# A trunk with two grouped MoE layers: passes of 64 tokens on two strips or 32 on four, freed tiles passed on by GpSimd, loops over experts

## What is computed

```python
def grouped_moe(h, router_w, router_b, w_gate, w_up, w_down):
    ...
    w_top, i_top = lax.top_k(in_group, TOP_K)
    w_top = w_top / w_top.sum(-1, keepdims=True)
    ...
    def expert_block(args):
        xb, e = args
        return (jax.nn.silu(xb @ w_gate[e]) * (xb @ w_up[e])) @ w_down[e]
```

## Time and profile before

| | |
|---|---|
| median of 3 runs | 1560.64 us (1557.62 to 1577.38) |
| the profiled execution | 1577.98 us, its span 1576.0 us |
| TensorE, matmuls | 1200.0 us busy (76%), 12964 |
| VectorE / ScalarE / GpSimd | 328.5 / 209.1 / 20.7 us busy |
| HBM | 492 MB read, 313 GB/s over the span |
| mean granted clock of TensorE | 0.833 |
| chain that ended last | PE 62%, DMA 19%, issue 13%, DVE 4% |
| MoE stages | about 230 to 738 us and 1036 to 1557 us of the span |

### The profile page before, as it was taken

One profiled execution on the slowest core, in us unless ns is written; L12 is line 12 of the kernel. 1 busy time (PEld: TensorE's weight loads), 2 busy tenths in 40 slices (PEclk: granted clock), 3 DMA queues, 4 the chain that ended last, 5 costly groups with the idle time before them and its releaser, 6 DMA issues.

```text
span 1576.0 us, 28851 instructions
## 1 busy us (share of the span) xinstructions
PE 1200.0 (76%) x12964; PEld 681.6 (43%) x12964; DVE 328.5 (21%) x838; ACT 209.1 (13%) x409; POOL 20.7 (1%) x53
## 2 busy tenths in 40 slices
PE   3799978667787478749798999677596887468746
PEld 1674344334443245324557565334253444235323
DVE  0595341001111011102400331521010110011004
ACT  0003001001111011102001121111011111111101
POOL 2100000000000000000000000000000000000000
PEclk8899968879888788878799867668798998689867
DMA  9729769999779998999733402159997699988980
GB/s 378 297 90 422 315 284 423 422 424 409 298 299 424 421 422 343 425 418 413 309 135 140 178 0 102 58 222 421 423 377 288 253 391 423 422 373 365 420 340 28
DMA packets 49384, 496.32 MB, mean 315 GB/s; under 512 B 4231, under 2 KB 4247, under 8 KB 8988
## 3 DMA queue, kind: packets, MB, share of 16 engines
q1 hardware_dynamic: 48176, 490.75, 75.3%
q10 hardware_dynamic: 684, 2.32, 0.4%
q0 software_dynamic: 320, 0.16, 0.1%
HBM read 492.17 MB, written 1.05 MB: 313 GB/s over the span
## 4 chain that ended last, share of the span: by engine, by line
PE 62%; DMA 19%; issue 13%; DVE 4%; ACT 1%; ACTq 0%; POOL 0%; DVEq 0%; POOLq 0%
PE PS L852 27%; DMA ring<-in_w_gate_dram 9%; PE PS L748 5%; DMA ring<-in_w_down_dram 5%; PE PS L1010 4%; PE PS L766 4%; DMA ring<-in_w_up_dram 3%; PE PS L887 3%; PE PS L682 3%; PE PS L830 3%; DMA work<-in_conv_ln_b_dram 2%; PE PS L1125 1%; PE PS L1128 1%; PE PS L1131 1%; PE PS L732 1%
## 5 line engine op out<-in xcount | busy, mean ns | idle before, releaser
L852 PE MATMUL PS<-ring,work 128*32 128x256 f32 x8064 | 517.1, 410 | 153.1 <-issue 118.4
L852 PEld LDWEIGHTS PS<-ring,work 128*32 128x32 f32 x8064 | 271.0, 117 | 367.3 <-issue 194.7
L830 PE MATMUL PS<-hs,work 128*32 128x256 f32 x752 | 60.4, 439 | 111.5 <-issue 109.8
L1352 DVE TENSOR_TENSOR work<-work,PS 128x256 f32<-128x256 f32 x47 | 19.8, 421 | 454.5 <-PE PS L852 454.5
L748 PE MATMUL PS<-ring,work 128*128 128x512 f32 x192 | 83.1, 593 | 0.5 <-ACT work L641 0.5
L830 PEld LDWEIGHTS PS<-hs,work 128*32 128x32 f32 x752 | 25.8, 121 | 132.6 <-issue 118.3
L887 PE MATMUL PS<-work 32*128 32x256 f32 x752 | 68.1, 484 | 14.9 <-issue 14.9
L682 PE MATMUL PS<-ring,crep 128*32 128x512 f32 x448 | 61.0, 694 | 18.9 <-DVE crep L1403 11.4
L1347 DVE COPY work<-PS 128x256 f32<-128x256 f32 x47 | 19.9, 424 | 244.0 <-PE PS L842 244.0
L526 ACT ACTIVATE work<-PS 128x256 f32<-128x256 f32 x47 | 18.1, 384 | 373.7 <-PE PS L830 373.7
L852 PE MATMUL PS<-work 128*32 128x256 f32 x960 | 59.7, 396 | 6.3 <-DMA work<-in_w_down_dram 6.3
(11 more groups left out here) (209 smaller groups left out, 853.8 us busy)
## 6 DMA issues: line engine op xcount, KB each, us to landing
ring<-in_w_gate_dram SPq DMA_DIRECT2D x64, 2048.0 KB, 25.5
ring<-in_w_up_dram SPq DMA_DIRECT2D x54, 2048.0 KB, 24.0
ring<-in_w_down_dram SPq DMA_DIRECT2D x54, 2048.0 KB, 21.3
ring<-in_w_ada_dram SPq DMA_DIRECT2D x24, 2048.0 KB, 19.0
work<-in_w_up_dram SPq DMA_DIRECT2D x10, 2048.0 KB, 18.9
work<-in_w_down_dram SPq DMA_DIRECT2D x10, 2048.0 KB, 24.9
ring<-in_w_pw_dram SPq DMA_DIRECT2D x6, 2048.0 KB, 39.3
ring<-in_w_ada_kv_dram SPq DMA_DIRECT2D x4, 2048.0 KB, 14.9
```

The source lines that it names most:

```text
L830: last = pe.matmul(PS[SLOTS * q:SLOTS * (q + 1), X_BANK, 0:QUART], G[:, t, :], hs[:, t, q * QUART:(q + 1) * QUART], start=(t == 0), stop=( ...
L852: last = pe.matmul(dst[SLOTS * s:SLOTS * (s + 1), :], rows[:, cc, SLOTS * q:SLOTS * (q + 1)], quarter(load + h, kk, KH)[:, QUART * s:QUART ...
L1352: dve.tensor_tensor(hh[kind.tile], hh[kind.tile], kind.up, ALU.mult).then_inc(hh_ready, 1)
```

## The change

A block has 64 slots (`large`) or 32 (`small`). An expert with b blocks of 32 by the old count runs `large` b // 2 times and, if b is odd, `small` once at the end. In `large` 64 tokens are the stationary operand and two column strips make 512 output columns each. In `small` 32 tokens are, on four strips: gate and up are made at once, two strips each; in the down product the strips split the columns in two and the contraction in two, and `combine` adds the parts up. TensorE's code holds one `large` and one `small` for each expert, for all experts in turn; ScalarE, VectorE and GpSimd have the bodies once a layer, in a loop over the experts (`Fori(0, E)`), and take the expert's columns by a register.

SP loads the tiles of an expert in the order gate 0, up 0, gate 1, up 1, down 0, down 1, and `large` and `small` use them in that order; the down tiles now have the row layout of the others. TensorE signals `half_done`, `gate_up_done`, `half_down` and `down_done` in every pass. GpSimd waits for each of them at an expert's last pass and raises `tile_free` by two, two, one and one, on which SP's loads into slots of expert tiles wait. The combine of the pass before always runs behind the first product or half, also at the first pass, where `yb` and `GWT` are cleared in advance; behind the last expert the tokens of a column of zeros are gathered once more. Four matmuls of one column close the sums. The diff, cut to its core (the removed bodies are printed above):

```diff
-SLOTS = 32
-STRIPS = 4
+SMALL = 32
+LARGE = 64
...
-    down_h = w_down.rearrange("l e (h q p c) f -> (l e) h p q c f", h=2, q=2, c=2)
+    down_h = w_down.rearrange("l e (h p k) f -> (l e) h p k f", h=2, p=P)
...
-                    sp.wait_ge(half_free, earlier[index] + 1)
+                    before_it = range(earlier[index] + 1)
+                    of_experts = sum(layer_of(i) is not None for i in before_it)
+                    if layer_of(earlier[index]) is None:
+                        sp.wait_ge(half_free, len(before_it) - of_experts)
+                    else:
+                        sp.wait_ge(tile_free, of_experts)
+                sp.dma_start(slot(index).rearrange("p (k f) -> p k f", k=source.shape[1]),
+                             source).then_inc(landed[home[index]], 16)
...
-                    for m, w in enumerate((gate_h, up_h, down_h)):
-                        for h in range(2):
-                            load(index + 6 * e + 2 * m + h, w[l * E + e, h])
+                    for m, (w, h) in enumerate(((gate_h, 0), (up_h, 0), (gate_h, 1), (up_h, 1),
+                                                (down_h, 0), (down_h, 1))):
+                        load(index + 6 * e + m, w[l * E + e, h])
...
+            def free_tiles(l):
+                pool.wait_ge(routed, l + 1)
+                with pool.Fori(0, E) as e:
+                    blocks = pool.value_load(blocks_i[0:1, bass.ds(e, 1)], min_val=1, max_val=SEQ // SMALL)
+                    pool.reg_add(passes, passes, (blocks + 1) // 2)
+                    for signal, tiles in ((half_done, 2), (gate_up_done, 2), (half_down, 1), (down_done, 1)):
+                        pool.wait_ge(signal, passes)
+                        pool.sem_inc(tile_free, tiles)
+
+            free_tiles(0)
             pool.wait_ge(spread_used, SPREADS0)
             for r, w in enumerate((ln_mix_g, ln_mix_b, ln_ffn_g, ln_ffn_b)):
                 pool.dma_start(lnrows[32 * r:32 * r + 1, :], w[1:2, :]).then_inc(rows_in[1], 16)
+            free_tiles(1)
...
+                def large():
+                    n = act.snap(n_act) + 1
                     act.wait_ge(gate_done, n)
+                    act.activation(hh, PS[:, GATE_BANK, :], ACT.Silu).then_inc(sil_ready, 1)
+                    take_x(n + 1)
                     act.wait_ge(hh_turned, n)
+                    act.activation(hhT, PS[:, HT_BANK, :], ACT.Copy).then_inc(hhT_copied, 1)
                     act.wait_ge(down_done, n)
+                    act.activation(yb, PS[:, DOWN_BANK, :], ACT.Copy).then_inc(yb_copied, 1)
                     act.reg_add(n_act, n_act, 1)
 
...
+                with act.Fori(0, E) as e:
+                    blocks = act.value_load(blocks_i[0:1, bass.ds(e, 1)], min_val=1, max_val=SEQ // SMALL)
                     with act.If(blocks > 1):
+                        with act.Fori(0, blocks // 2):
+                            large()
+                    with act.If(blocks % 2 > 0):
+                        small()
...
+                def sum_x(n):
+                    pe.wait_ge(G_built, n + l)
                     for t in range(TT):
+                        for h in range(2):
+                            last = pe.matmul(PS[LARGE * h:LARGE * (h + 1), X_BANK, :], G[:, t, :],
+                                             hs[:, t, h * HALF:(h + 1) * HALF], start=(t == 0), stop=(t == TT - 1),
+                                             tile_position=(0, LARGE * h), skip_group_check=True)
                     last.then_inc(X_summed, 1)
...
+                def combine(n):
+                    pe.wait_ge(yb_copied, n + l + 1)
+                    pe.wait_ge(GWT_copied, n + l + 1)
                     for t in range(TT):
+                        for h in range(2):
+                            pe.matmul(PS[:, 2 * t + h, :], GWT[LARGE * h:LARGE * (h + 1), t * P:(t + 1) * P],
+                                      yb[LARGE * h:LARGE * (h + 1), :], start=False, stop=False,
                                       skip_group_check=True)
+                def columns(tile, k, half):
+                    return quarter(tile, k, KH)[:, half * BANK:(half + 1) * BANK]
+                def large(load):
+                    n = pe.snap(n_pe) + 1
+                    def product(tile, h, bank, signal):
+                        arrived(tile)
+                        for kk in range(KH):
+                            for half in range(2):
+                                last = pe.matmul(PS[LARGE * half:LARGE * (half + 1), bank, :],
+                                                 XT[:, kk, LARGE * h:LARGE * (h + 1)], columns(tile, kk, half),
+                                                 start=(h == 0 and kk == 0), stop=(h == 1 and kk == KH - 1),
+                                                 tile_position=(0, LARGE * half), skip_group_check=True)
+                        if signal is not None:
+                            last.then_inc(signal, 1)
+                    pe.wait_ge(XT_copied, n + l)
+                    product(load, 0, GATE_BANK, None)
+                    combine(n - 1)
+                    product(load + 1, 0, UP_BANK, half_done)
+                    product(load + 2, 1, GATE_BANK, gate_done)
+                    product(load + 3, 1, UP_BANK, gate_up_done)
+                    sum_x(n + 1)
+                    pe.wait_ge(hh_ready, n)
...
+                    last.then_inc(hh_turned, 1)
+                    turn_gw(n)
+                    turn_x(n + 1)
                     pe.wait_ge(hhT_copied, n)
+                    for h in range(2):
...
+                    pe.wait_ge(GWT_copied, n + l + 1)
                     pe.reg_add(n_pe, n_pe, 1)
+                def small(load):
+                    n = pe.snap(n_pe) + 1
+                    pe.wait_ge(XT_copied, n + l)
+                    for h in range(2):
+                        arrived(load + 2 * h)
+                        arrived(load + 2 * h + 1)
+                        for kk in range(KH):
+                            for strip in range(4):
+                                last = pe.matmul(PS[SMALL * strip:SMALL * (strip + 1), GATE_BANK, :],
+                                                 XT[:, kk, LARGE * h:LARGE * h + SMALL],
+                                                 columns(load + 2 * h + strip // 2, kk, strip % 2),
+                                                 start=(h == 0 and kk == 0), stop=(h == 1 and kk == KH - 1),
+                                                 tile_position=(0, SMALL * strip), skip_group_check=True)
+                                if h == 1 and kk == strip == 0:
+                                    last.then_inc(gate_done, 1)
+                        last.then_inc((half_done, gate_up_done)[h], 1)
+                        if h == 0:
+                            combine(n - 1)
                     sum_x(n + 1)
+                    pe.wait_ge(hh_ready, n)
+                    turn_gw(n)
...
+                    last.then_inc(hh_turned, 1)
                     turn_x(n + 1)
                     pe.wait_ge(hhT_copied, n)
+                    for h in range(2):
+                        arrived(load + 4 + h)
+                        for kk in range(KH):
+                            for half in range(2):
+                                strip = 2 * half + kk % 2
+                                last = pe.matmul(PS[SMALL * strip:SMALL * (strip + 1), DOWN_BANK, :],
+                                                 hhT[:, kk * LARGE + SMALL * h:kk * LARGE + SMALL * (h + 1)],
+                                                 columns(load + 4 + h, kk, half),
+                                                 start=(h == 0 and kk < 2), stop=(h == 1 and kk >= KH - 2),
+                                                 tile_position=(0, SMALL * strip), skip_group_check=True)
+                        last.then_inc((half_down, down_done)[h], 1)
+                    pe.wait_ge(GWT_copied, n + l + 1)
+                    pe.reg_add(n_pe, n_pe, 1)
                 pe.wait_ge(routed, l + 1)
                 first = pe.snap(n_pe) + 1
                 sum_x(first)
                 turn_x(first)
                 for e in range(E):
+                    blocks = pe.value_load(blocks_i[0:1, e:e + 1], min_val=1, max_val=SEQ // SMALL)
                     with pe.If(blocks > 1):
+                        with pe.Fori(0, blocks // 2):
+                            large(index + 6 * e)
+                    with pe.If(blocks % 2 > 0):
+                        small(index + 6 * e)
+                combine(pe.snap(n_pe))
+                pe.wait_ge(XT_copied, pe.snap(n_pe) + (l + 1))
+                for b in range(4):
+                    last = pe.matmul(PS[:, b, 0:1], ident[0:1, 1:2].to_broadcast([1, P]), hs[0:1, 0, 0:1],
+                                     start=False, stop=True, skip_group_check=True)
+                last.then_inc(y_ready, 1)
...
+                def slots_of(start, n):
```

(43 more changed lines are left out.)

305 lines of the change are left out of this document (65 added, 240 removed).

## The result

| | |
|---|---|
| kernel before, same chip | 1569.01 us median of 4 runs (1557.62 to 1581.04) |
| changed kernel | 1447.81 us median of 4 runs (1443.01 to 1466.66) |
| ratio | 0.924, 95% interval 0.9133 to 0.9346 |
| profiled executions | 1577.98 us before, 1443.01 us after (span 1441.3) |

The change gains 121 us. The sign and the mechanism of the holes were right, and the gain was 39 us larger than forecast. Runs of either kernel that are otherwise alike scatter by 20 to 30 us around these medians; what makes most of it is part of what follows.

The account below looks back on a forecast made before the run. The MoE stages were taken as bound by weight transfers, except where TensorE, stalled at jumps, freed tiles late. Layer 2 -56, layer 1 -45 and costs gave -91; 9 less on the median made -82, 1478 us, range 1455 to 1528.

Parts of the forecast that it names:

- the mechanism of the holes: MoE stages: TensorE, late at taken branches, frees tiles late, so the ring fills and transfers lose 34 and 47 us.
- I assume half of that lies in the waits that go: Profiled execution was 17 us over the 1560.64 median; half put on the removed waits, so 9 us less gain.
- The next stage ... is otherwise untouched: Stage after layer 1's experts: starts earlier by layer 1's gain of 45 us, with nothing else changed.
- Costs of 10 us: Jumps before layer 2's hole +4, last product at half clock +4, memsets, spare-column clearing and first-block delays +2.
- Layer 2, -56: Layer 2's MoE stage: one hole of 8 us, last landing 1493, end at 1501 instead of 1556.9.
- tile 29: Last weight tile of expert 4, counting from 0; landings forecast from it at 4.97 us a tile: 354.2 and 1156.6.
- at nothing: Costs taken as zero: ScalarE and VectorE loops over experts, GpSimd's relay of freed tiles, the down tiles' new layout.
- Layer 1, -45: Layer 1's MoE stage: no hole, last landing 682, ada tiles end at 704 instead of 748.6.
- The waits for issue of 12 us: TensorE's waits at taken branches in the MoE stages; forecast: no wait for issue of 9 to 13 us remains.
- C: Slower rival: two 64-column strips do not overlap, 433 ns a matmul, `large` 51 us; +90, 1650 us; chance 0.06.
- 1.3 us on the average: Price of TensorE's jump past a body of 265 instructions, between bounds of 0 to 1.4 and 6.2 us.
- Rival B: Jumps still stall, `large` 35.6 and `small` 25.6 us, TensorE sets the pace; middle -50, 1510 us; chance 0.24.

Follow-up runs that it names:

- experiment 13: Kernel before, with attention's product that spreads the forget sums run over all 128 array rows (112 zeros) instead of 16: 1537.21 us, ratio 0.9801 to the kernel before.
- experiment 11: Changed kernel, with attention's product that spreads the forget sums run over 128 array rows instead of 16: 1435.69 us, ratio 0.9117.
- 14: Changed kernel with the forget-sum product on 128 rows, once more, on the same chip as the kernel before with that edit: 1434.56 us, ratio 0.9139.
- the pair: Kernel before and changed kernel, both with the forget-sum product on 128 rows, on one chip: 1537.21 and 1434.56 us.
- experiment 8: Changed kernel with the loops over experts on VectorE, ScalarE and GpSimd unrolled: 1455.59 us, ratio 0.93.
- experiments 3: Changed kernel with three dead `large` bodies behind a third, never taken branch in each expert: 1589.46 us, ratio 1.0107.
- experiment 4: Changed kernel with one dead `large` body behind a third branch in each expert: 1516.92 us, against 1454.69 for the changed kernel on that chip.
- experiment 5: Changed kernel without `large`: every expert runs `small` once per block of 32, in a loop on each engine: 1525.31 us, ratio 0.9706.
- 12: Changed kernel with an extra product of 128 rows and 512 columns per attention head, result unused: 1454.84 us.
- experiment 1: Kernel before with TensorE's branches resolved while the program is built, so it never jumps: 1468.56 us, ratio 0.9341.

## Why the prediction was wrong

The forecast gain was 82 us and the measured one 121. The step that failed is what the prediction made of the stage between the layers: it put that stage's clock at nothing, and laid the scatter that this clock makes on the waits (points 1 and 2, 27 of the 39 us between forecast and result). By the prediction's own steps:

1. **"I assume half of that lies in the waits that go, so 9 less is gained on the median."** The runs show the 17 us between the profiled execution and the median in attention's clock, not in the waits. The stages with the waits took 511.6 and 521.3 us in that execution and 511.7 and 521.0 in the one of experiment 13, while its heads took 80.1 us at 0.64 and there 50.0 at 1.00. With the clock held, the median gain equals the one on profiles (102.6 and 102.8). The sum lost 9 us here.
2. **"The next stage ... is otherwise untouched": wrong by 12 to 18 us.** The code is untouched, but its clock was lower more often in the kernel before: the edit of experiment 11 takes 31.3 us off the kernel before and 19.0 off the changed one (1454.69 to 1435.69), which is 12 us; the first chip's 121 against the 103 of experiments 13 and 14 leaves 18. Part of the 18 is which runs the medians rest on: the forecast counts from 1560.64, the median of three runs, and the fourth makes it 1569.01. The lowest of all 46 runs of the kernel before, 1553.36, is still 21 us above its lowest with the edit; the changed kernel's 1443.01 is 10 above its own. Why the clock fell more in the one kernel is open; nothing here shows that the change had a part in it. The row was there to read: 80 us of back-to-back matmuls with a clock of 0.64 in a stage that the prediction never opened.
3. **Costs of 10 us: none of them showed.** Jumps cost 4.2 us, as much as I had said, but in layer 1 and inside its term. The last product of layer 2 did not run at half clock: its 32 matmuls took 7.09 us, as in the middle of the stage; its combine waited 0.70 us, for ScalarE, and the jump in front of it stayed behind that copy. The sum gets back 7 us and not 10, since the router's clock took 3.2 in the pair; that is no cost of the change.
4. **Layer 2, -56: it was -61.9.** By the landings in the trace of the changed kernel, tile 29 landed 118.8 us behind the router's end (120.9 before), and the 66 tiles behind it took 333.2 us where the sum has 336, with a hole of 5.4 us and not 8: together 5 of the 6 us. The plateaus moved 427 GB/s, 4.91 us a tile and not 4.97; the down tiles' layout, which I had "at nothing", may be a part of it. The hole is shorter because a `large` is 26.2 us and not 28: `combine` took 1.9 (I kept 1.7 to 3.5; the row halves of the array overlap too). `small` is 16 us and not 18.
5. **Layer 1, -45: it was -44.1** on the pair, where the router's clock took 2.2, and 748.6 - 701.7 = 47 on the profiles of before and after. Right in size, in part by luck: the 66 tiles behind tile 29 took 326.6 us (328 in the sum), with the 4.2 us of jumps in them that the sum had put elsewhere; faster tiles made up for these.

Points 1, 3 and 4 are 9 + 7 + 6, less 1 for point 5, and point 2 is 18.

What was right. The waits for issue of 12 us are gone, there is one hole, behind layer 2's expert 6, and TensorE waits for tiles in most experts. The last tiles landed at 678.9 and, on the old axis, 1487.7 us, for 682 and 1493. The loops on ScalarE and VectorE cost nothing (experiment 8). C fell at once: 218 ns a matmul. The Trainium skill (TensorEngine Tiling (Array Packing), Tiling Modes) has the two tiles of 64 columns run in parallel; the trace agrees.

**The jumps were right in sum and half right in reason.** I took 1.3 us on the average and a target "partly on its way". TensorE takes 29 jumps past a body (20 experts of one block jump past `large`, 9 of two past `small`) and waits 27.3 us for issue, 0.94 us each. But they are not small waits evenly spread:

```profile
399.09 3.65 PE L857 MATMUL PS<-ring,work 128*64 128x512 f32 x16 [0.52 <-issue]
...
430.95 5.71 PE L901 MATMUL PS<-ring,work 128*32 128x512 f32 x32 [5.67 <-issue]
...
453.92 6.17 PE L901 MATMUL PS<-ring,work 128*32 128x512 f32 x32 [4.75 <-issue]
...
572.81 6.45 PE L901 MATMUL PS<-ring,work 128*32 128x512 f32 x32 [8.77 <-issue]
```

At 430.95 and 572.81 an expert of two blocks is followed by one of one block, two jumps in a row; at 453.92 stands a single one; at 399.09 a single one into `large`. All seven waits lie in layer 1; why layer 2 shows none, with the same code, is open. With 16 or 26 us of work for 29.5 us of transfer there is room for a jump of 3 to 13 us. So most may stand behind a wait for a tile and not be seen; the trace cannot tell a hidden stall from none. Rival B was half true: some jumps still stall, and what decides is that the stall fits into the slack. By experiments 3 and 4 the slack is used up when another 32 jumps are added. The price rises with the distance. In the same place, from a two-block to a one-block expert, TensorE waits 5.7 and 8.8 us with no dead body, 14.0 to 14.5 with one and 20.0 to 22.3 with three (four jumps in a row instead of two). The Trainium skill (Runtime: NRT & Kernel Launch, Instruction fetch mechanics) has a branch outside the held code wait for a DMA. That agrees in kind with these waits, with more instruction blocks fetched (81 packets; 112 and 145 with dead bodies; 173 before), and with experiment 5's free jump back. It gives no price, and the price here was taken while the DMA engines were full of weights; whether they set it was not tried.

What stays open: what decides, from run to run, when the clock falls in the heads, and why it fell more often in the kernel before. With the old product the profiles show values from 0.57 to 0.97. That the product on all 128 rows holds the clock up is shown by 11, 13 and 14; that an extra full product does is seen in the one profile of 12 and in its narrow runs. Whether it is the rows at work or the shorter time from product to product was not separated.

## What to carry to other kernels

A taken branch past code costs by how much it skips and by how many such branches follow each other: give the body that is skipped few instructions, put no two skips in a row, and see that the loop has slack against its transfers. Before an execution's excess over the median is put down to the part that one is changing, read the granted clock of every long stretch of back-to-back matmuls, the untouched ones too. Where the clock falls in such a stretch, try to widen a thin product with zeros: here it cost no time and brought 19 and 31 us.

## What was not expected of the hardware

- TensorE's granted clock fell from 2.4 to 1.2 GHz (0.48 to 0.79 us for the same matmuls) within uninterrupted work on products of 16, 64 and 128 rows; with the 16-row ones on 128 rows it was 1.00 in all three profiles taken.
- A product over 128 rows behind one over 16 rows starts 0.41 us after it and takes 0.49 us; behind one over 128 rows 0.32 and 0.39 us.
- Four jumps in a row past dead code cost up to 14.5 us with one dead body and 22.3 us with three; a jump back over one body of some 265 instructions showed no wait.
- Behind a jump that waited, TensorE can wait a second time some 5 us later in straight code: 14 times in experiment 4, up to 4.5 us.
- The same bytes in 41192 instead of 49384 packets moved at 425 instead of 422 GB/s in one window of one profile each; the older layout also showed 424 in experiment 1.
